# Delta-rule inverse: the transposed copy by transposes instead of a second product

## The reference

```
a = where(strict, einsum(k_beta, k) * decay, 0)
m = a + eye
u = triangular_solve(m, v * beta)          # lower, unit diagonal
w = triangular_solve(m, k_beta * exp(gc))
```

## Time and profile before

| what | value |
|---|---|
| runs | 4094.25, 4095.87, 4096.15 us; median 4095.87 |
| profiled execution | span 4092.7 us from first to last instruction; its time with what lies around the span is not listed apart |
| mean granted TensorE clock | 0.909 of full speed |
| TensorE products, busy | 3457.7 us, 84% |
| VectorE busy | 1412.5 us, 35% |
| ScalarE busy | 841.8 us, 21% |
| POOL busy | 1435.3 us, 35% |

### The profile page before, as it was taken

The page is one execution under the profiler, slowest core; times in us unless marked ns, Lnnn a source line. Parts: engine busy times, 40 slices in busy tenths (PEclk is TensorE's granted clock), DMA queues, the critical chain, the costliest instruction groups (busy, mean ns, idle before and its releaser), DMA issues.

```text
span 4092.7 us, 61740 instructions
## 1 busy us (share of the span) xinstructions
PE 3457.7 (84%) x21792; PEld 3089.2 (75%) x21792; DVE 1412.5 (35%) x2231; ACT 841.8 (21%) x1657; POOL 1435.3 (35%) x1088
## 2 busy tenths in 40 slices
PE   6978887777889987999987788887687899799997
PEld 5967767535659987999977676784374799799996
DVE  2066663255531222111122666614553412211112
ACT  3133332232111112000022333313312111210001
POOL 0444442002205543444424444320131255254443
PEclk8988898877799998999988999987787999899998
DMA  4201111111102211222211111111111122121221
GB/s 159 75 29 42 41 41 62 55 41 50 58 27 72 77 66 48 72 72 70 75 64 51 43 41 41 41 62 54 41 55 49 37 77 72 41 77 67 71 73 67
DMA packets 62782, 240.94 MB, mean 59 GB/s; under 512 B 6960, under 2 KB 6960, under 8 KB 61488
## 3 DMA queue, kind: packets, MB, share of 16 engines
q1 hardware_dynamic: 60336, 224.77, 15.9%
q10 hardware_dynamic: 1728, 12.36, 0.8%
q0 software_dynamic: 576, 2.10, 0.1%
HBM read 234.48 MB, written 4.72 MB: 58 GB/s over the span
## 4 chain that ended last, share of the span: by engine, by line
PE 69%; DVE 16%; issue 6%; DVEq 4%; ACT 2%; POOL 1%; ACTq 1%; POOLq 1%; DMA 0%; SPq 0%
PE ps_G L583 26%; PE ps_GPM L583 25%; DVE whi_room L1564 3%; PE ps_GPM L614 3%; DVE outs L1636 2%; PE ps_M L967 2%; DVE outs L1632 2%; PE ps_G L852 1%; DVE small L1756 1%; PE ps_M L909 1%; PE ps_M L891 1%; PE ps_M L664 1%; PE ps_M L995 1%; DVE big L1787 1%; DVEq L1453 1%
## 5 line engine op out<-in xcount | busy, mean ns | idle before, releaser
L1973 POOL CAST w_hi<-ring 128x1024 fp32r<-128x1024 f32 x296 | 309.0, 1044 | 1620.8 <-PE ps_G L583 1002.4
L1975 POOL TENSOR_TENSOR w_lo<-ring,w_hi 128x1024 fp32r<-128x1024 f32 x296 | 740.3, 2501 | 51.1 <-issue 9.1
L583 PE MATMUL ps_G<-room_a,w_hi 128*128 128x320 f32 x1984 | 457.9, 320 | 100.1 <-DVEq L1453 65.4
L583 PE MATMUL ps_GPM<-room_a,w_hi 128*128 128x320 f32 x1984 | 437.5, 309 | 0.0
L583 PEld LDWEIGHTS ps_G<-room_a,w_hi 128*128 128x128 f32 x1984 | 348.5, 197 | 103.0 <-issue 103.0
L583 PE MATMUL ps_G<-room_b,w_hi 128*128 128x320 f32 x1408 | 368.4, 314 | 26.4 <-DVEq L1453 26.4
L583 PE MATMUL ps_G<-room_o,w_hi 128*128 128x320 f32 x1280 | 337.2, 313 | 45.6 <-DVEq L1453 45.6
L583 PE MATMUL ps_GPM<-room_b,w_hi 128*128 128x320 f32 x1408 | 361.4, 309 | 0.0
L583 PE MATMUL ps_GPM<-room_o,w_hi 128*128 128x320 f32 x1280 | 332.9, 309 | 0.0
L583 PEld LDWEIGHTS ps_GPM<-room_a,w_hi 128*128 128x128 f32 x1984 | 331.8, 188 | 0.0
L2027 POOL TENSOR_TENSOR outs<-big,con 128x512 f32<-128x512 f32 x168 | 207.7, 1237 | 350.1 <-DVEq L1602 230.9
(11 more groups left out here) (393 smaller groups left out, 6006.8 us busy)
## 6 DMA issues: line engine op xcount, KB each, us to landing
ring<-in_W SPq DMA_DIRECT2D x416, 512.0 KB, 3.2
big<-in_INV ACTq DMA_DIRECT2D x2, 1664.0 KB, 6.6
par<-in_PARAMS ACTq DMA_DIRECT2D x2, 1646.0 KB, 7.8
big<-in_FWD ACTq DMA_DIRECT2D x2, 1632.0 KB, 8.3
x<-in_X SPq DMA_DIRECT2D x1, 2560.0 KB, 8.8
out_Y<-h SPq DMA_DIRECT2D x1, 2560.0 KB, 7.6
con<-in_CONSTS SPq DMA_DIRECT2D x1, 1364.0 KB, 11.6
sc<-in_HYCS ACTq DMA_DIRECT2D x2, 578.5 KB, 3.7
```

The costliest lines, as they stand in the source:

```text
L583: m = pe.matmul(ap, w[wi][:, k, n0:n0 + P], acts[ai][k][:, a:b], start=(k == 0 and i == 0), stop=(k == chunks - 1 and i == 2))
L1973: nc.gpsimd.tensor_copy(hi, raw)
L1975: nc.gpsimd.tensor_tensor(wlo[:, slot * UNIT:(slot + 1) * UNIT], raw, hi.bitcast(F32), ALU.subtract)
```

## The change

In levels 1 to 5 the E product and its subtraction go. Instead, TensorE transposes the updated `X_` into PSUM (fills T1 to T5) and VectorE copies that into `XT`. The transposes stand in TensorE's queue after the P products of the next level and before its D products; the copies stand in VectorE's queue after the three subtractions of the level and before the taps. Level 6 needs `XT` alone and keeps its E product. The number of PSUM fills per head stays the same.

```diff
--- before.py
+++ after.py
@@ delta_fills
-        for g, _, _ in GROUPS:
-            names += [f"D{lev}_{g}"] if lev < NLEV - 1 else []
-            names += [f"E{lev}_{g}"]
+        names += [f"T{lev - 1}_{g}" for g, _, _ in GROUPS] if lev > 1 else []
+        names += [f"{'D' if lev < NLEV - 1 else 'E'}{lev}_{g}" for g, _, _ in GROUPS]
@@ TensorE, after the P products of a level
+                        if lev > 1:
+                            for g, first, n in G3:
+                                ap, fl = f(f"T{lev - 1}_{GROUPS[g][0]}")
+                                for c in range(n):
+                                    m = pe.transpose(ap[:, c * P:(c + 1) * P], X_[:, first + c, :], ident)
+                                m.then_inc(fl, 1)
                         for g, first, n in G3:
                             pe.wait_ge(p_ready.sem, p_ready.at(Q, 3 * (lev - 1) + g + 1))
                             if lev > 1:
                                 pe.wait_ge(xt_ready.sem, xt_ready.at(Q, 3 * (lev - 1) + g + 1))
-                            if lev < NLEV - 1:
-                                ap, fl = f(f"D{lev}_{GROUPS[g][0]}")
-                                for c in range(n):
-                                    m = pe.matmul(ap[:, c * P:(c + 1) * P], XT[:, first + c, :], PS[:, first + c, :],
-                                                  start=True, stop=True)
-                                m.then_inc(fl, 1)
-                            ap, fl = f(f"E{lev}_{GROUPS[g][0]}")
+                            ap, fl = f(f"{'D' if lev < NLEV - 1 else 'E'}{lev}_{GROUPS[g][0]}")
                             for c in range(n):
-                                m = pe.matmul(ap[:, c * P:(c + 1) * P], PS[:, first + c, :], XT[:, first + c, :],
+                                a_, b_ = (XT, PS) if lev < NLEV - 1 else (PS, XT)
+                                m = pe.matmul(ap[:, c * P:(c + 1) * P], a_[:, first + c, :], b_[:, first + c, :],
                                               start=True, stop=True)
                             m.then_inc(fl, 1)
@@ VectorE, a level
+                            old = X_ if lev < NLEV - 1 else XT
+                            ap, fr = f(f"{'D' if lev < NLEV - 1 else 'E'}{lev}_{GROUPS[g][0]}")
...
+                            tt(old[:, m3, :], old[:, m3, :], ap[:, 0:n * P].rearrange("p (a b) -> p a b", a=n),
                                ALU.subtract).then_inc(fr, 1)
-                            dve.drain().then_inc(xt_ready.sem, 1)
+                            dve.drain().then_inc((x_ready if lev < NLEV - 1 else xt_ready).sem, 1)
+                        if lev < NLEV - 1:
+                            for g, first, n in G3:
+                                ap, fr = f(f"T{lev}_{GROUPS[g][0]}")
+                                nc.vector.tensor_copy(XT[:, first:first + n, :],
+                                                      ap[:, 0:n * P].rearrange("p (a b) -> p a b", a=n)).then_inc(fr, 1)
+                                dve.drain().then_inc(xt_ready.sem, 1)
```

More of the change, by code:

```diff
@@ L1626, in _ @@
                             m3 = slice(first, first + n)
[L1627 to L1636, removed]
-                               ALU.subtract).then_inc(fr, 1)
-                            dve.drain().then_inc(xt_ready.sem, 1)
+                            old = X_ if lev < NLEV - 1 else XT
+                            ap, fr = f(f"{'D' if lev < NLEV - 1 else 'E'}{lev}_{GROUPS[g][0]}")
+                            if lev == 1:
+                                dve.wait_ge(x0_ready.sem, x0_ready.at(Q, g + 1))
+                            tt(old[:, m3, :], old[:, m3, :], ap[:, 0:n * P].rearrange("p (a b) -> p a b", a=n),
+                               ALU.subtract).then_inc(fr, 1)
+                            dve.drain().then_inc((x_ready if lev < NLEV - 1 else xt_ready).sem, 1)
[5 more added lines that the diff above has]
+                                dve.drain().then_inc(xt_ready.sem, 1)
                         if lev == 1:
```

## The result

The changed kernel takes 4201.11 us (median of four runs, 4196.97 to 4205.39) against 4095.55 before (four runs; with the first three it was 4095.87): slower, ratio 1.0262 with a 95% interval of 1.0247 to 1.0276. Forecast were 4197 and a range of 4128 to 4243.

What follows compares the result with a forecast made beforehand. The prediction took VectorE's in-order queue to bound levels 2 to 4, and POOL level 1. Per head, 5.6 us of waits plus 7.1 of lower clock made 12.7, 101.6 for eight: 4095.9 to 4197, range 4128 to 4243.

Steps and rivals of the forecast that it cites:

- The place of the copies: Levels 2 to 4: VectorE's copies wait for transposes queued behind the next level's P, 1.33 us lost per level.
- What comes back from POOL: Levels 2 to 4: POOL starts earlier, slowing only the first tap by 0.3 us; net +1.4 us for the three.
- Level 1: Level 2's P products wait for POOL, and VectorE's copies now wait behind them: +3.8 us per head.
- Level 5: Its copies end at 5.97 us, so level 6 starts at 6.18 instead of 5.82: +0.36 us per head.
- The clock: TensorE's longer pause under the taps brings the 1.2 GHz level on the P-to-transpose path: 7.1 us per head.
- The rival with the lower clock on every new path: 1.2 GHz throughout the new paths in the level loop: 18.4 us per head in all, 4243 us; chance 13%.
- that with none: TensorE's clock stays up throughout the level loop: 4141 us, down to 4132 with cheaper copies; chance 16%.
- The sum: Level loop: 5.6 us at the higher clock plus 7.1 for the clock, 12.7 per head, 101.6 for eight.
- What I said would show it: Copies idle about 1.5 us in levels 2 to 5, 6 in level 1; loop 50 to 60; clock under 1.00.

Runs made afterwards that it cites:

- the product kernel: Changed kernel plus ten identity products nothing reads, behind the D products of levels 1 to 5, filling TensorE's pause: 4139.19 us, ratio 1.0115.
- kd late: Changed kernel with POOL's ten TENSOR_SCALAR into kd moved from before level 2's mask to behind level 6's: 4138.85 us, ratio 1.0108.
- the fill kernels: Changed kernel plus 20 unread TensorE passes behind the D products of levels 1 to 5: as identity products 4139.19 us, as transposes 4143.79.

## Why the prediction was right

*The place of the copies.* Right to 0.1 us. At the higher clock (the product kernel) P starts 0.87 after the first subtraction and the copy 3.84, forecast 0.86 and 3.75; levels 2 to 4 take 9.36, 9.55 and 9.35, forecast 9.42, 9.58 and 9.42. The order alone, without another instruction, brings 84 us back.

*What comes back from POOL.* Right: no tap is slowed, and levels 2 to 4 come out 0.03 to 0.07 under the forecast.

*Level 1.* Right in cause, shown by kd late; 14.2 at the higher clock against 13.8 forecast.

*Level 5.* Mis-sized: 6.62 against 6.18. The third copy starts 0.56 behind the second, not 0.21, as the instruction in that place did before; I had not looked at it. After and before:

```profile
316.55 0.42 DVE L1638 COPY outs<-ps_GPM 128x256 f32<-128x256 f32 x1 [0.56 <-issue]
```

```profile
300.58 0.42 DVE L1636 TENSOR_TENSOR outs<-outs,ps_M 128x256 f32<-128x256 f32 x1 [0.56 <-issue]
```

*The clock.* The least certain term, and the one whose mechanism the fill kernels settle. Forecast 1.5 in each of levels 2 to 5 and 1.1 in level 1, 7.1 a head. Change minus product kernel, in the mean of the heads: 1.5, 2.3, 1.9 and 1.6, and in level 1 1.2 (1.4 without the product kernel's eighth head): 8.5 to 8.7. Right in kind and too small by some 1.5. The rival with the lower clock on every new path (12.8) and that with none are both out.

*The sum.* The loop grew by 15.0 a head where the steps gave 12.7: 6.5 at the higher clock (the product kernel) against 5.6, too small in levels 1 and 5, and 8.5 by the clock against 7.1. Over eight heads that is 19 us too little, so that the time still came out within 4 us is partly luck. The forecast took a microsecond in a level for one in the span and had nothing outside the loop, where 9 us came back; and the profiled execution, 4205.39, is the slowest of the four, 4.3 above their median. From a head's loop to the next, up to 1.4 us was gained, and 2.7 between the layers. What gained it is open. The granted clock between the first and the second head's loop is 0.89 where it was 0.86; but in the last two such gaps the kernel before has 0.89 too, and they take 60.9 and 61.0 against 59.8 and 59.6, so the clock is not the whole of it.

*What I said would show it.* The copies wait 3.1 to 4.2 us in levels 2 to 5, not about 1.5: I had written down the wait at the higher clock, though my own sum had the lower one in it. In level 1 they wait 7.2 to 7.8, where I had said 6. The rest is as told: 60 us a head, the upper end of the 50 to 60, a clock of 0.83, no slow taps.

## What to carry to other kernels

Before swapping an operation for a cheaper one, ask where its input stands in the other engine's queue: a copy that waits behind the next stage's products holds up everything written behind it on its own engine. A saved product is worth nothing where it was hidden, and a pause that it leaves on TensorE can slow the next products, so price the pause too. Put a copy that must wait on an engine whose next work is not ready earlier: with the transposes ahead of P, the kernel was 0.6% slower with the copies on VectorE and 1.9% faster with them on ScalarE.

## What was not expected of the hardware

Useless work made the kernel faster: 100 added passes a head took 60 us off, with the granted clock in the loop up from 0.83 to 1.00. Transposes kept TensorE at the 2.4 GHz level as well as products did (1.00 in the loop with 800 of them).
